# A two-layer decoder step on one core: query norm beside the last values, forget-gate weights in a buffer of their own, heads' high halves two per request

## The reference, cut to what matters

```python
for l in range(DEPTH):                                  # DEPTH = 2
    hn = _modnorm(x, norm_mix_g[l], sh1, sc1)
    if l < N_A_LAYERS:                                  # layer 0
        out, ... = _rglru_block(hn, ...)
    else:                                               # layer 1
        q = (hn @ fa_wq[j]).reshape(bsz, t, N_HEADS, HEAD_DIM)
        o = _forgetting_attention(q, k_all, v_all, cq, cum, q_pos, k_pos)
        out = o.reshape(bsz, t, hw) @ fa_wo[j]
    x = x + (1 + g1) * out
    hn = _modnorm(x, norm_ffn_g[l], sh2, sc2)
    out, ... = _conv_ffn(hn, ...)
    x = x + (1 + g2) * out
    if l == N_A_LAYERS - 1:                             # after layer 0
        hk = _modnorm(x, kv_norm_g, kv_shift, kv_scale)
        proj = hk @ kv_w                                # 1024 x (1024 + 1024 + 16)
        k_new, v_new = proj[..., :hw], proj[..., hw:2 * hw]
        lf_new = log_sigmoid(proj[..., 2 * hw:] + kv_b_f)
        cum = cumsum(concat(lf_past, lf_new))           # bias of the attention
```

## Time and profile before

| what | value |
|---|---|
| median of three runs | 3229.92 us |
| the profiled execution, its own time | 3229.8 us |
| its span (first to last instruction) | 3228.3 us |
| mean granted TensorE clock | 0.975 |
| TensorE busy | 94% of the span |
| VectorE, ScalarE, GpSimd busy | 43%, 27%, 35% |
| DMA over the span | 91 GB/s |

### The profile page before, as it was taken

One profiled execution on the slowest core, in us unless ns is written; L12 is line 12 of the kernel. 1 busy time (PEld: TensorE's weight loads), 2 busy tenths in 40 slices (PEclk: granted clock), 3 DMA queues, 4 the chain that ended last, 5 costly groups with the idle time before them and its releaser, 6 DMA issues.

```text
span 3228.3 us, 48968 instructions
## 1 busy us (share of the span) xinstructions
PE 3026.4 (94%) x19142; PEld 2833.4 (88%) x19142; DVE 1383.6 (43%) x2021; ACT 884.3 (27%) x1475; POOL 1121.9 (35%) x571
## 2 busy tenths in 40 slices
PE   5999989899999999998998988888899999999996
PEld 4978859799999999997998866657899999999995
DVE  6345381543434444446103165642444435344345
ACT  3143170241312112122212145541241312121121
POOL 1312205433333333332332255524333333333331
PEclk9999989999999999999999999999999999999998
DMA  5634612111111111111543564664111111111111
GB/s 213 251 132 154 232 63 78 52 46 46 41 43 45 45 39 45 45 39 40 167 146 145 153 140 99 178 264 177 39 46 46 40 45 45 45 40 45 45 39 68
DMA packets 99464, 295.58 MB, mean 92 GB/s; under 512 B 14000, under 2 KB 15408, under 8 KB 99104
## 3 DMA queue, kind: packets, MB, share of 16 engines
q1 hardware_dynamic: 85616, 244.52, 22.9%
q10 hardware_dynamic: 13744, 49.61, 4.5%
HBM read 253.98 MB, written 40.10 MB: 91 GB/s over the span
## 4 chain that ended last, share of the span: by engine, by line
PE 66%; issue 10%; DVE 4%; POOL 3%; ACT 2%; DMA 1%; ACTq 0%; SPq 0%; POOLq 0%; DVEq 0%
PE PS L630 57%; PE PS L919 2%; POOL WH L566 2%; PE PS L902 2%; POOL WL L569 1%; PE PS L886 1%; PE PS L887 1%; ACT PX L1320 1%; DMA KB<-in_cache_k 1%; DMA X<-in_xT 0%; PE PS L648 0%; ACT PT L1310 0%; PE PS L933 0%; DVE X L1913 0%; PE PS L965 0%
## 5 line engine op out<-in xcount | busy, mean ns | idle before, releaser
L566 POOL TENSOR_TENSOR WH<-WRAW,ZERO 128x1024 fp32r<-128x1024 f32 x214 | 410.3, 1917 | 1818.6 <-ACTq L1052 1237.1
L630 PE MATMUL PS<-HH,WH 128*128 128x342 f32 (+1 forms) x3144 | 699.3, 331 | 8.3 <-POOL WL L569 4.7
L630 PE MATMUL PS<-HL,WH 128*128 128x342 f32 (+1 forms) x3144 | 698.5, 330 | 0.0
L630 PE MATMUL PS<-HH,WL 128*128 128x342 f32 (+1 forms) x3144 | 696.3, 330 | 0.0
L630 PEld LDWEIGHTS PS<-HH,WH 128*128 128x128 f32 x3144 | 556.8, 190 | 16.9 <-issue 15.8
L630 PEld LDWEIGHTS PS<-HL,WH 128*128 128x128 f32 x3144 | 560.4, 189 | 0.2
L630 PEld LDWEIGHTS PS<-HH,WL 128*128 128x128 f32 x3144 | 559.0, 189 | 1.6
L569 POOL TENSOR_TENSOR WL<-WRAW,WH 128x1024 fp32r<-128x1024 f32 x214 | 545.6, 2550 | 16.8
L1686 DVE SCALAR_TENSOR_TENSOR FC<-FU,FCW,FC 128x1026 f32<-128x1026 f32 x96 | 239.1, 2491 | 571.5 <-ACT FC L1178 571.5
L630 PE MATMUL PS<-AH,WH 128*128 128x342 f32 (+1 forms) x1152 | 257.3, 332 | 6.3 <-DVE AL L1704 5.0
L630 PE MATMUL PS<-AH,WL 128*128 128x342 f32 (+1 forms) x1152 | 255.9, 330 | 0.0
(11 more groups left out here) (275 smaller groups left out, 3552.7 us busy)
## 6 DMA issues: line engine op xcount, KB each, us to landing
WRAW<-in_wstream SPq DMA_DIRECT2D x214, 512.0 KB, 3.5
MS<-in_mod_w SPq DMA_DIRECT2D x96, 512.0 KB, 6.8
KB<-in_cache_k SPq DMA_DIRECT2D x32, 512.0 KB, 8.8
VB<-in_cache_v SPq DMA_DIRECT2D x32, 512.0 KB, 8.2
K<-k_split SPq DMA_DIRECT2D x48, 256.0 KB
Q<-q_split SPq DMA_DIRECT2D x48, 256.0 KB
out_kv<-STG ACTq DMA_DIRECT2D x16, 545.0 KB, 3.2
MU<-in_mod_w SPq DMA_DIRECT2D x16, 512.0 KB, 12.2
```

The lines of the kernel that those rows point to most:

```text
L566: pool.tensor_tensor(WH[:, u, :], WRAW[:, u, :], ZERO[:].broadcast_to([P, UNIT]), ALU.add).then_inc(hi.sem, 1)
L630: mm = pe.matmul(PS[:, o:o + hi - lo], lhs(n), rhs[:, k, lo:hi], start=first and n == 0 and m == 0, stop=last and n == len(kts) - 1 and m ...
```

## The change

Three parts. The forget-gate weights leave the stream of units: SP loads their 16 columns into a small buffer LFW, GpSimd splits them between the splits of key units 1 and 2, and TensorE uses 16-column stationary tiles; the unit of zeros is no longer loaded or split. The query norm is scaled into tiles TQ of its own; VectorE's part no longer waits for the stores, ScalarE's high halves stand between the last copies of the values, and the last turn of values moves into the first two query units. ScalarE hands over the heads' high halves two per request, in requests 0 to 3.

```diff
+    LFW = at("LFW", O_R3 + 60800, [P, KT, NH])
+    LFH = at("LFH", O_R3 + 60800 + 4 * KT * NH, [P, KT, NH], F32R)
+    LFL = at("LFL", O_R3 + 60800 + 8 * KT * NH, [P, KT, NH], F32R)
+    TQ = kv("TQ", [P, 2, T])
...
-        def weights(first, units, peel):
+        def weights(first, units, peel, left_out=0):
...
-                    sp.wait_ge(S["split_done"], first + i * 2 + u - 1)
+                    sp.wait_ge(S["split_done"], first + i * 2 + u - 1 - left_out)
...
-        for n, v in enumerate((2, 3, 0, 1)):
-            sp.wait_ge(S["split_done"], logs + n - 1)
-            sp.dma_start(WRAW[:, n % 2, :], I["wstream"][logs + v]).then_inc(S[f"w_raw{n % 2}"], 16)
-        weights(logs + 4, UNITS_1 - logs - 4, False)
+        sp.dma_start(LFW[:], I["wstream"][logs].rearrange("p (k c) -> p k c", k=KT)[:, :, 0:NH]).then_inc(S["lf_w"], 16)
+        weights(logs + U_LF, UNITS_1 - logs - U_LF, False, U_LF)
...
-        order = [("AA", RT), ("PD", KT), ("AA", GC), (group, NG - 1), ("DD", KT // 4), ("AA", 1), ("DD", 1), ("AA", KT - 1),
+        order = [("AA", RT), ("PD", KT), ("AA", GC), (group, NG - 1), ("DD", KT // 4), "logs", ("AA", KT),
                  ("AA", KT // 2 - 1), None, ("AA", 1), ("DD", KT // 2), ("AA", GC), (group, NG - 1),
...
+            if item == "logs":
+                pool.wait_ge(S["lf_w"], 16)
+                pool.tensor_tensor(LFH[:], LFW[:], ZERO[:].unsqueeze(1).broadcast_to([P, KT, NH]), ALU.add)\
+                    .then_inc(S["lf_w_hi"], 1)
+                pool.wait_ge(S["lf_w_hi"], 1)
+                pool.tensor_tensor(LFL[:], LFW[:], LFH[:].bitcast(F32), ALU.subtract).then_inc(S["lf_w_split"], 1)
+                continue
...
             for k, units in [(k, (0, 1)) for k in range(2, SHARED)] + [(k, (u,)) for u in range(2) for k in range(SHARED, KT)]:
+                if between and k == 3 and units[0] == 0:
+                    between()
...
         two_units()
-        pe.wait_ge(split.sem, split.next())
+        pe.wait_ge(S["lf_w_split"], 1)
         pe.wait_ge(free[0].sem, free[0].next())
-        job(0, tiles(WH, 0), tiles(WL, 0), HH, HL, range(KT)).then_inc(ready[0], 1)
-        split.next()
+        for k in range(KT):
+            for m, (w_, x) in enumerate(((LFH, HH), (LFH, HL), (LFL, HH))):
+                for c, (lo, hi) in enumerate(PIECES):
+                    mm = pe.matmul(PS[0:NH, SLOT[0] + 512 * c:SLOT[0] + 512 * c + hi - lo], w_[:, k, :], x[:, k, lo:hi],
+                                   start=k == 0 and m == 0, stop=k == KT - 1 and m == 2)
+        mm.then_inc(ready[0], 1)
...
-        turn_values(1)
-
-        two_units(roots_in_psum=False)
+        two_units(roots_in_psum=False, between=lambda: turn_values(1))
...
-        with rounds(act, KT // 2 - 1, {ready[0]: 1, ready[1]: 1, me: 2, v_turned: 2, v_kept: 2}
+        with rounds(act, KT // 2 - 2, {ready[0]: 1, ready[1]: 1, me: 2, v_turned: 2, v_kept: 2}
...
+        value_unit(0, KT - 2)
+        values_split(1, KT - 3)
+        value_unit(1, KT - 1)
+        high(3, range(2))
+        values_split(0, KT - 2)
+        high(3, range(2, 4))
         values_split(1, KT - 1)
+        high(3, range(4, KT))
         for n in range(2):
             act.wait_ge(out[n].sem, out[n].now() + 16)
             act.wait_ge(vout[n].sem, vout[n].now() + 16)
         act.wait_ge(S["lf_out"], 16)
-        norm(3, sums=False)
...
         output_hi(0)
+        output_hi(1)
         weighed_request(0)
...
-            output_hi(k)
+            for p in (2 * k, 2 * k + 1):
+                if p < KT:
+                    output_hi(p)
             weighed_request(k)
...
             got(0)
-            dve.sem_inc(S["used_dve"], 2)
...
+        dve.wait_ge(S["lf_out"], 16)
+        dve.wait_ge(S["cum_out"], 32)
+        norm(3, sums=False)
         for n in range(2):
             dve.wait_ge(S[f"kv_out{n}"], KT * 16 + 16)
             dve.wait_ge(S[f"v_out{n}"], KT // 2 * 16 + 16)
-        dve.wait_ge(S["lf_out"], 16)
-        dve.wait_ge(S["cum_out"], 32)
-        norm(3, sums=False)
```

More of the change, by code:

```diff
@@ L352, in trunk @@
         y_hi y_ready x_done x_back rst_out ffn_in ffn_out f_conv f_gelu f_prod f_hi act_ready
[L353 removed]
+        kv_out0 kv_out1 k_hi split_out0 split_out1 v_staged v_turned v_kept v_out0 v_out1 lf_w lf_w_hi lf_w_split lf_e lf_ready lf_out cum_out q_ready
         const_rows kq_in0 kq_in1 kq_in2 kq_in3 x_kept x_again v_in0 v_in1 s_ready max_done exp_done inv_done p_normed turned0 turned1 pt_act pt_dve weighed
@@ L548, in _ @@
         sp.dma_start(X[:], XSC).then_inc(S["x_again"], 16)
-        weights(UNITS_1 + 2, UNITS_2 - 2, False)
+        weights(UNITS_1 + 2, UNITS_2 - 2, False, U_LF)
     @block.gpsimd
@@ L575, in _ @@
         group = "AA" + "DD" * (KT // 4) + "AA" * (GC - 1)
-        order = [("AA", RT), ("PD", KT), ("AA", GC), (group, NG - 1), ("DD", KT // 4), ("AA", 1), ("DD", 1), ("AA", KT - 1),
+        order = [("AA", RT), ("PD", KT), ("AA", GC), (group, NG - 1), ("DD", KT // 4), "logs", ("AA", KT),
                  ("AA", KT // 2 - 1), None, ("AA", 1), ("DD", KT // 2), ("AA", GC), (group, NG - 1),
                  ("DD", KT // 4 - 1)]
-        assert 2 + sum(len(o[0]) * o[1] for o in order if o) == UNITS_1 + UNITS_2
+        assert 2 + sum(len(o[0]) * o[1] for o in order if isinstance(o, tuple)) == UNITS_1 + UNITS_2 - U_LF
         def attention():
@@ L639, in unit_job, with two_units @@
             job(u, tiles(WH, u), tiles(WL, u), xh, xl, range(KT), fresh=fresh).then_inc(ready[u], 1)
-        def two_units(roots_in_psum=True):
+        def two_units(roots_in_psum=True, between=None):
             def part_of(k, u, pieces, lows):
@@ L1074, in kept, with high @@
             ins.then_inc(S["act_root"], 1)
-        def high(n):
-            for k in range(KT):
+        def high(n, tiles=range(KT)):
+            for k in tiles:
                 sh = NORMS[n][0] + k
@@ L1090, in high @@
                     act.wait_ge(tn.sem, tn.next())
-                    ins = act.activation(HH[:, k, 0:S0], TN[:, k % 2, 0:S0], ACT.Identity, bias=MOD[:, sh, 0:1])
+                    ins = act.activation(HH[:, k, 0:S0], (TQ if n == 3 else TN)[:, k % 2, 0:S0], ACT.Identity,
+                                         bias=MOD[:, sh, 0:1])
                 ins.then_inc(S["act_hi"], 1)
@@ L1453, in scaled @@
             sc = NORMS[n][1] + k
-            STT(TN[:, k % 2, 0:S0], X[:, k, 0:S0], MOD[:, sc, 0:1], RS[:, 0:S0], ALU.mult, ALU.mult).then_inc(S["dve_tn"], 1)
+            STT((TQ if n == 3 else TN)[:, k % 2, 0:S0], X[:, k, 0:S0], MOD[:, sc, 0:1], RS[:, 0:S0], ALU.mult, ALU.mult)\
+                .then_inc(S["dve_tn"], 1)
         def scaled_samples(n):
@@ L1468, in lowered @@
             sh = NORMS[n][0] + k
-            ins = STT(HL[:, k, 0:S0], TN[:, k % 2, 0:S0], MOD[:, sh, 0:1], HH[:, k, 0:S0].bitcast(F32), ALU.add, ALU.subtract)
+            ins = STT(HL[:, k, 0:S0], (TQ if n == 3 else TN)[:, k % 2, 0:S0], MOD[:, sh, 0:1], HH[:, k, 0:S0].bitcast(F32), ALU.add, ALU.subtract)
             if k == 0:
```

## The result

The changed kernel takes 3211.86 us (median of four runs, 3207.27 to 3213.53) beside 3229.75 us for the kernel before on the same chip: a ratio of 0.9945 (95% interval 0.993 to 0.996). Two later series of the same kernel gave 3214.31 and 3213.66 us. The forecast was 3213.4 us, 0.5% faster. The profiled execution took 3213.09 us, with a span of 3211.6 us, against 3228.3 us before: 16.7 us less (17.9 by the medians), where 16.5 were forecast.

A forecast was written before the change was run, and what follows sets the result against it. TensorE, busy 3026.4 of 3228.3 us, was taken as the bound, with gains only from its waits and lower clock. A 4.83 + B 6.4 + C 5.31 = 16.5 us off 3229.8, on the median 3213.4 us; range 3209.5 to 3220.

The forecast's parts named there:

- The reading of the bound: Whole kernel: TensorE busy 3026.4 of 3228.3 us; gains must come from its 202 us standing still or lower-clock stretches.
- the step on the clock: Key unit 2: the idle stretch shrinks to 1.76 us, so the clock holds and 1.94 us of half clock go.
- the rival of 54.7 us: Forget-gate matmuls: narrow stationary tile slows all 72 to 54.7 us instead of 12.0, total 3256 us; chance 0.04.
- Its two terms of loss: Query units: 1.75 us lost to half clock; last transposes and ScalarE's copy delay high tiles 4 to 7 and VectorE's chain.
- the step on the port: Query units' start: VectorE's first lowering waits 1 us beside GpSimd's split, costing nothing; if GpSimd yielded, restart 1.06 us later.
- so the half-clock stretch that now follows goes too: 1.97: Output projection's first unit: after a 1.8 us idle stretch it takes 12.04 us instead of 14.01, gaining 1.97 us.
- Rival 2: Clock falls also over the 1.8 us stretches of A and C: 3217.3 us; chance 0.14.
- the 2.42 us row: Profile row cited for A's clock: an idle stretch of 2.42 us kept the clock at 1.00.
- rival 1: Query units: the clock holds over B's 3.72 us wait, total 3211.7 us; chance 0.17.
- rival 3: Query stage: B's gain is eaten by its new order or by late kept input or keys, 3219.8 us; chance 0.08.
- rival 4: Output projection: GpSimd or weights late for another reason, split starts as before, 3218.7 us; chance 0.07.
- One sign named beforehand as bad: Requests: the forecast is wrong if a key or page wait there grows; no size given.

The follow-up runs named there:

- after: The changed kernel with all three parts, against the kernel before: profiled execution 3213.09 us; median 3211.86 us, ratio 0.9945.
- the control: The changed kernel run again unaltered, as measure for the kernels that undo one part each: 3214.31 us, ratio 0.9956 to the kernel before.

## Why the prediction was right, and the term that was not

**The reading of the bound** held. What the three parts gained came out of TensorE's waits and the clock behind them; C lets GpSimd end its subtractions some 29 us earlier, counted from the requests' first key products, and about 3 us of that reached the end.

**A** was put at 4.83 us and gave 5.11. The wait ended by VectorE's read of the logits was forecast at 1.76 us and is 1.56; the unit behind it runs at 1.00, as the step on the clock said (1.94 forecast, 1.87 measured); the 72 forget-gate matmuls take 12.07 us where 12.29 lay between their start and the old wait (1532.48 and 1544.77), so the narrow tile costs nothing. That refutes the rival of 54.7 us. The gap of 0.27 us ahead of these matmuls was not in the sum.

**B** was put at 6.4 us and gave 6.70 against before. The 0.3 us more are a matter of the mark: the prediction ended the two units at 1763.88 and the table counts to query unit 2's start, 1764.17. The wait was forecast at 3.72 us and is 3.67, ended by GpSimd; the restart was forecast 8.58 us earlier and is 8.62 earlier as counted from the end of the last value unit; the stretch was forecast at 32.4 us and is 32.36. Its two terms of loss were tried one by one: 1.75 us of half clock measure 1.5, and the chain through ScalarE's copy 0.8 where the steps had let it set the end of the units. In the step on the port VectorE was to wait, not GpSimd, and it did: 2.51 us instead of 1.28, beside a split of 2.35 us that had begun 0.93 us before. The Trainium skill ("SBUF — State Buffer", section "SBUF: two separate sides") says that of a VectorE operation with two SBUF inputs and a GpSimd operation that reads SBUF the one that starts first keeps the shared ports for its whole length and the other blocks; these rows agree to 0.2 us, since 1.28 us behind the split's end at 1725.59 is 1726.87, and VectorE ended at 1726.68.

**C** was put at 5.31 us and gave 3.31. The wait did what the steps said: the weights' landing sets the split, VectorE's last subtraction sets the restart, 2.97 us earlier (3.34 forecast; the 0.2 us by which the heads were to come forward did not show, and the wait is 2.00 us, not 1.8; with those 0.2 us the prediction's own times give 1.62, from 2203.18 to 2204.80). The step that failed is the next one, "so the half-clock stretch that now follows goes too: 1.97". The projection took 101.37 us instead of 101.71: 0.34 us. In the eight profiles with C and the old start of the projection it took 101.25 us or more seven times, and once, without A, 99.85, so the 1.97 us are a chance and not a term to count on. Rival 2 came true in this half, with that one exception, and not in A's. The argument compared lengths of idle stretches (1.8 us against the 2.42 us row) and that row does not carry it: behind those 2.42 us came 1 us of transposes and the next wait, so nothing there showed what a dense stretch behind it would get.

Of the other rivals, the clock did not hold over B's wait (rival 1: 0.57 us a pair behind it), B's gain was not eaten by its new order (rival 3: neither the units nor the stretch behind them give it back), and C did move the split (rival 4).

**The total** came out right by chance as to the last 2 us: C fell short by 2.0, A and B gave 0.6 more, and stretches the change hardly touches gave 1.6. In its three series the changed kernel's median gained 17.9, 14.4 and 16.4 us, around the 15.1 that A, B and C sum to. One sign named beforehand as bad did appear: TensorE's waits for request keys grew from 5.3 to 6.9 us in the profile of after. In the eleven other profiles they lie between 4.1 and 6.8 us whatever the order of the heads, so the change isn't shown to be their cause.

## What to carry to other kernels

Where an engine waits for a buffer, look up what is late next before counting the wait as gained: here GpSimd's split gave way to a PSUM read (A), to another split (B) and to the last heads (C), and each of the three left 1.6 to 3.7 us. Count a wait's clock as a term of its own, only with a row in which the same kind of work stands on both sides of the gap, and from more than one profile: behind C's wait it fell in seven of eight. If work can't be moved into the wait, products that nobody reads can hold the clock: 22 of them were worth 1.5 us and made nothing later.

## What the runs showed of the hardware that was not expected

The length of an idle stretch alone does not decide what the clock does behind it. TensorE's 1.56 us ahead of key unit 2 left it at 1.00 in all eleven profiles with part A, and the 2.3 or 3.7 us ahead of the query units were followed by half clock in all nine profiles that have such a wait unfilled. In between the same wait went both ways: behind 2.00 us ahead of the output projection the clock was at half for a while in seven profiles and stayed at 1.00 in one. Waits for keys in the requests went both ways too. In each of the twelve other profiles one of 2.8 us or more was followed by half clock; in the timeline of after two passed without it:

```profile
2167.82 1.07 PE L946 MATMUL PS<-KB,QX 128*32 128x256 f32 x16 [3.16 <-DMA KB<-in_cache_k]
...
2177.99 1.07 PE L946 MATMUL PS<-KB,QX 128*32 128x256 f32 x16 [3.00 <-DMA KB<-in_cache_k]
```

Both ran at full pace, and the granted clock was 1.00 from 2167.82 until the wait of 2.00 us; before, an idle stretch of 3.00 us at the same kind of work was followed by 0.54. The fall did not always lie at the same distance from the restart either: some 0.7 us behind it in the run that starts query unit 0 first, 1.1 us behind it in after's projection, while the control's projection was at half clock from its first matmul. What decides this stays open. What is shown is the counterpart: with the gap filled, by real or by unread products, the granted clock stayed at 1.00 behind it, in two profiles at the query units and in three at the projection.

A stationary tile of 16 columns keeps the pace of one of 128 in this type: three matmuls of it start 0.50 us after the last three, and 72 take 12.07 us, against 12.04 with 128 columns.

Two profiles of the same kernel, after and the control, had a mean granted clock of 0.976 and 0.973 and spans of 3211.6 and 3214.8 us. That is enough to hide a change of 3 us in the medians: without C the median rose by 1.1 us, while the stretch is 1.4 to 4.1 us longer than in the eight profiles with C.
